# Rotary swap by ScalarE copies instead of a TensorE product, and a new placement of the buffers in SBUF

## The chip, the cores and the metric

The kernel runs on one core of a Trainium2 chip. The metric is the device time of one execution in microseconds (us). An execution works on both input sequences, through both layers of the encoder.

## What is computed

The reference is an encoder of two layers on two sequences of 256 tokens, with 1024 features. Each layer has one input projection; its columns feed a windowed attention with rotary positions and a two-sided state-space mixer (SSD). An output projection, a layer norm, a gated MLP and a second layer norm follow. All data is float32. The part that the change touches is the rotation:

```python
def rope(x):                      # x (B,S,H,64), for 8 query heads and 2 key heads
    ang = arange(s)[:, None] * inv_freq[None, :]
    cos, sin = cos(ang), sin(ang)
    x1, x2 = x[..., :32], x[..., 32:]
    return concatenate([x1 * cos - x2 * sin, x2 * cos + x1 * sin], -1)

def hybrid_layer(h, ...):
    proj = h @ w_in
    q, k, v, z, xbc, dt_raw = split(proj)
    attn_out = window_attention(rope(q), rope(k), v, sink)
    ...                           # conv, SiLU, SSD, gate, RMS norm
    h = layer_norm(ALPHA * h + concat(attn_out, ssd_out) @ w_out)
    gate, val = split(h @ w_up)
    return layer_norm(ALPHA * h + (silu(conv(gate)) * val) @ w_down)
```

## The kernel before, in words

**Units.** The weights of a layer are cut into 105 units of 128x1024: unit 0 is the time step (dt), 1 the keys, 2 the values, 3 to 6 the queries (two heads each), 7 to 18 the columns that go through the convolution, 19 to 26 the gate z, 27 to 38 the output projection, 39 to 82 the MLP's first product, 83 to 104 its second. SyncE loads them into a ring of five (`raw`). ScalarE rounds each to float32r (`whi`, L554), VectorE takes the rest (`wlo`, L1113), which overwrites `raw`. Each float32 product is three float32r matmuls: high by high, high by low, low by high. The activations are kept in the same two parts (`hhi`/`hlo`, `ahi`/`alo`, `uhi`/`ulo`).

**Two forms of the big product.** `by_columns` (L778 to L780) has 128 columns of `whi` or `wlo` as the stationary operand and 512 tokens of `hhi` or `hlo` as the moving one: 24 matmuls a unit, all into one PSUM bank. `by_rows` (L821 to L823; output projection and the MLP's second product) has 128 tokens of `ahi`, `alo`, `uhi` or `ulo` as the stationary operand and 512 columns of `whi` or `wlo` as the moving one. `first_units` runs the first two units after a layer norm with 256 tokens at a time.

**Order.** `mixer_schedule` writes one list of steps, which every engine walks and from which it takes its own: G (a unit on TensorE), E (ScalarE empties that unit's bank), S (split of the unit four ahead), ROT (rotation), DTT and SP (softplus of dt), AA, AO and SM (the decay sums, their matmuls and their split), VT (transposes of the values), AS, AM, AX, AD, AN, AP, AV (attention, from step 8 on), F, F2 and SILU (convolution taps and SiLU). The engines run apart and meet at semaphores. G(i) waits until unit i-2 has been emptied. VT takes the PSUM bank of AA, so it waits until VectorE has written `own_z` from it (L1289).

**Rotation before.** For each of five tiles of 128 rows (two heads), ScalarE copies the bank to `qk` (L651). TensorE multiplies `qk` by the 128x128 matrix `rot` (L975; a plain float32 matmul, which the profile counts as two), which puts minus the upper 32 rows of each head where the lower are, and the lower where the upper are. VectorE multiplies that product by the sines into `ropet` (L1328), `qk` by the cosines (L1329), and adds (L1331). `rope_done` counts finished tiles. ROT stands one step behind its unit.

**Buffers.** They are allocated one after another. Without an alignment asked for, each starts at the next multiple of 32 bytes. In the program before, in bytes per partition: `cn` (constants) at 16512, `avg` at 21792, `raw`/`wlo` at 23488, `whi` at 43968, `hhi` at 64448, `hlo` at 80832, `big_i` at 100096, the two arenas at 101632 and 118016. The other tiles (`ahi`, `alo`, `uhi`, `ulo`, `own_w`, `heads`, `qk`, ...) lie at whole multiples of 1024 bytes in an arena. All slots and slices of the big operands step by multiples of 512 bytes. So `whi`, `wlo`, `hhi`, `hlo` start 960 bytes past a multiple of 2048, the tiles at even KB of the arenas 1280 past one, and `avg` 32 past a multiple of 64.

Of the kernel before, what the change touches and what calls it, by code (L numbers as in the profile page):

```python
# [61 lines left out]
def _columns(table, widths):  # L62
    at = 0
    for name, w in widths:
# [11 lines left out]
                     ("before", P), ("rot", P), ("cos", SEQ), ("sin", SEQ),  # L76
# [28 lines left out]
def mixer_schedule():  # L105
    steps = []
    for n in range(U_OUT):
        i = n - A0
        steps += [("G", n), ("E", n)]
        if 0 <= i < 8:  # L110
            steps += [("AS", i), ("AM", i)]
        if 0 <= i - 2 < 8:
            steps += [("AV", i - 2)]
        if n == 1:
            steps += [("DTT", 0), ("SP", 0)]
        if n == 3:
            steps += [("AA", 0), ("AO", 0), ("SM", 0)]
        if n - 1 == U_V:
            steps += [("VT", 0)]
        if n - 1 == U_K:  # L120
            steps += [("ROT", 4)]
        if U_Q <= n - 1 < U_Q + 4:
            steps += [("ROT", n - 1 - U_Q)]
        steps += [("S", n + AHEAD)]
        if 0 <= i < 8:
            steps += [("AX", i)]
        steps += [("F", n)]
        if 0 <= i < 8:
            steps += [("AD", i), ("AN", i)]
        if n == 15:  # L130
            steps += [("MV", 0), ("MV", 1)]
        if n == 16:
            steps += [("MV", 2), ("MV", 3)]
        if U_CONV <= n < U_Z:
            steps += [("F2", n)]
        if 0 <= i - 1 < 8:
            steps += [("AP", i - 1)]
        j = n - 1 - U_CONV
        if 4 <= j < N_CONV:
            steps += [("T", j)]  # L140
        if 12 <= n < 16:
            steps += [("CB", n - 12)]
        if U_CONV <= n < U_Z:
            steps += [("SILU", n - U_CONV)]
            if n - U_CONV >= 4:
                steps += [("XS", n - U_CONV)]
        for k in PROD_SLOTS.get(n, []):
            steps += prod_steps(k)
        if n == 23:
            steps += [("SG", i) for i in range(3)]  # L150
        if n == 24:
            steps += [("SG", 3)]
        if n == 26:
            steps += [("SG", i) for i in range(4, 7)] + [("SQ", c) for c in range(4)]
# [27 lines left out]
def trunk(nc, x_in, units, pm_d, pf_d, cn_d, gb_d, h_d, y_d):  # L182
    ctx = ExitStack()
    with ctx:
# [7 lines left out]
        cn = sb("cn", [P, CN_W])  # L192
        avg = sb("avg", [P, P])

        st = sb("st", [P, NBLK, 4])
        pm = sb("pm", [P, PM_W])
        pf = sb("pf", [P, PF_W])
# [5 lines left out]
        dt = sb("dt", [P, NBLK, 32])  # L203
        cum_a = sb("cum_a", [P, TOK])
        neg_a = sb("neg_a", [P, 32])
        ast = sb("ast", [P, 2, 6, QPK])

        big_i = sb("big_i", [P, P], F32R)
        cut = sb("cut", [P, 2, P], F32R)
# [6 lines left out]
        base = nc.sbuf_base - ARENA_KB * KB  # L216

# [79 lines left out]
        proj_copied, rope_sin, rope_done = sem("proj_copied"), sem("rope_sin"), sem("rope_done")  # L297
# [33 lines left out]
        for what, i in SCHED:  # L331
# [15 lines left out]
            elif what == "ROT":  # L347
                aux(("ROT", i), [(rope_sin, 5, (i + 1) % 5 + 1)])
            elif what == "AP":
                yy(("AP", i, 0), [(pt_done, 8, i + 1)])  # L350
                yy(("AP", i, 1), [(pt_done, 8, i + 1)])
            elif what == "AV":
                aux(("AV", i), [(al_done, 8, i + 1)])
            elif what == "RS" and i == 0:
                aux(("RS", 0), [(rms_std, 1, 1)], False)
            elif what == "SD":
                aux(("SD", i), [(y_sum, 8, i + 1)])
# [189 lines left out]
        def _(act):  # L547
# [81 lines left out]
            for L in range(DEPTH):  # L629
                act.wait_ge(pm_loaded, L * 16 + 16)  # L630
                for what, i in SCHED:
# [15 lines left out]
                    elif what == "E" and i < U_Z:  # L647
                        m = i - U_K
                        act.wait_ge(unit_used, L * UNITS + i + 1)
                        dst = zt[:] if i == U_V else qk[:, 4 if i == U_K else i - U_Q, :]  # L650
# [122 lines left out]
        def _(pe):  # L773
# [94 lines left out]
            for L in range(DEPTH):  # L868
                for what, i in SCHED:
# [102 lines left out]
                    elif what == "ROT":  # L972
                        pe.wait_ge(proj_copied, L * 6 + (1 if i == 4 else 3 + i))
                        wait_aux_free(pe, L, (what, i))
                        mm(ps[:, aux_bank((what, i)), :], cst("rot"), qk[:, i, :], start=True,  # L975
                           stop=True).then_inc(aux_full, 1)
# [129 lines left out]
        def _(dve):  # L1106
# [103 lines left out]
            for L in range(DEPTH):  # L1210
                dve.wait_ge(pm_loaded, L * 16 + 16)
                for what, i in SCHED:
# [107 lines left out]
                    elif what == "ROT":  # L1320
                        wait_aux_full(dve, L, (what, i))
# [3 lines left out]
                        r = ps[:, aux_bank((what, i)), :].rearrange("p (b s) -> p b s", b=NSEQ)  # L1325
                        if n:
                            dve.wait_ge(rope_done, L * 5 + n)
                        V.tensor_tensor(tt, r, cst("sin").unsqueeze(1).broadcast_to((P, NSEQ, SEQ)), ALU.mult).then_inc(rope_sin, 1)  # L1328
                        chain(V.tensor_tensor(x, x, cst("cos").unsqueeze(1).broadcast_to((P, NSEQ, SEQ)), ALU.mult))  # L1329
                        dve.wait_ge(rope_sin, L * 5 + n + 1)  # L1330
# [131 lines left out]
def constants():  # L1462
# [3 lines left out]
    rot = np.zeros((P, P), np.float32)  # L1466
    for m in range(P):
        if m % HEAD < HEAD // 2:
            rot[m + HEAD // 2, m] = -1.0
        else:  # L1470
            rot[m - HEAD // 2, m] = 1.0
    freq = np.float32(10000.0) ** (-np.arange(0, HEAD, 2, dtype=np.float32) / np.float32(HEAD))
    ang = np.arange(SEQ, dtype=np.float32)[None, :] * freq[np.arange(P) % (HEAD // 2)][:, None]
    row = np.arange(P)
    is_a = (row // 16) % 2 == 1
# [5 lines left out]
        "after": k > q, "before": k < q, "rot": rot, "cos": np.cos(ang), "sin": np.sin(ang),  # L1481
# [77 lines left out]
```

## Time and profile before

| | us |
|---|---|
| median of three runs | 1392.52 (1392.41 to 1395.36) |
| the profiled execution | 1392.02 |
| its span, first to last instruction | 1390.2 |
| busy in the span: PE (matmul) | 1355.3 (97%) |
| PEld (weight load) | 1102.4 |
| VectorE (DVE) | 754.6 |
| ScalarE (ACT) | 559.6 |
| GpSimd (POOL) | 202.4 |

A matmul's record reaches from its start to the end of its way through the array, and the next one starts before it ends. So the busy time of PE says that it is rarely idle, not how fast it goes. How fast is read from the distance between starts, or from the count of matmuls in a window in which PE doesn't wait.

### The profile page before, as it was taken

How to read it: one execution, taken by the hardware profiler on the slowest of the kernel's cores; microseconds unless marked ns; L12 is line 12 of the kernel's file. 1: busy time of each engine (PE TensorE's matmuls, PEld its weight loads, DVE VectorE, ACT ScalarE, POOL GpSimd, SP SyncE). 2: the span in 40 equal slices, each digit the busy share in tenths (PEclk: the TensorE clock that was granted, in tenths of full speed). 3: DMA queues.
4: the chain of work that ended last, by engine and by line, in shares of the span. 5: the costliest groups of instructions: out<-in, count | busy, mean ns of one | idle time of the engine just before them, and what ended most of it. 6: DMA issues, size and time to landing. Idle time of an engine off the chain costs nothing.

```text
span 1390.2 us, 16378 instructions
## 1 busy us (share of the span) xinstructions
PE 1355.3 (97%) x6740; PEld 1102.4 (79%) x6740; DVE 754.6 (54%) x1006; ACT 559.6 (40%) x851; POOL 202.4 (15%) x119
## 2 busy tenths in 40 slices
PE   7999999999999999999999999999999999999997
PEld 6777778788888888888777777877788888888886
DVE  5777776655544444332266877667464444443225
ACT  5355544425433333311253655444263333333112
POOL 3013400162000000060020224002520000002300
PEclk9999999999999999999999999999999999999999
DMA  4421111251333333333224221124233333333332
GB/s 160 152 76 60 48 60 46 63 193 48 117 95 93 105 91 98 114 106 91 76 95 137 61 62 61 46 61 161 67 95 103 91 103 95 93 104 121 91 94 103
DMA packets 33786, 129.95 MB, mean 93 GB/s; under 512 B 3792, under 2 KB 3952, under 8 KB 32560
## 3 DMA queue, kind: packets, MB, share of 16 engines
q1 hardware_dynamic: 33552, 128.61, 29.4%
q8 instruction: 54, 0.88, 0.3%
q0 software_dynamic: 160, 0.29, 0.1%
q14 instruction: 20, 0.16, 0.0%
HBM read 122.60 MB, written 6.29 MB: 93 GB/s over the span
## 4 chain that ended last, share of the span: by engine, by line
PE 86%; DVE 6%; ACT 4%; issue 2%; DMA 1%; POOL 1%; DVEq 0%; SPq 0%; ACTq 0%; POOLq 0%
PE ps L778 17%; PE ps L780 17%; PE ps L779 17%; PE ps L821 8%; PE ps L823 8%; PE ps L822 8%; PE ps L1015 2%; DVE cv L1226 1%; PE ps L995 1%; ACT junk L559 1%; PE ps L1046 1%; PE ps L1056 1%; DVE hb L1128 1%; DVE wlo L1113 1%; PE ps L1036 1%
## 5 line engine op out<-in xcount | busy, mean ns | idle before, releaser
L778 PE MATMUL ps<-hhi,whi 128*128 128x512 f32 (+1 forms) x1200 | 464.9, 387 | 11.4 <-DVE hlo L1161 10.5
L779 PE MATMUL ps<-hlo,whi 128*128 128x512 f32 (+1 forms) x1200 | 455.8, 380 | 0.0
L780 PE MATMUL ps<-hhi,wlo 128*128 128x512 f32 (+1 forms) x1200 | 455.7, 380 | 0.0
L1113 DVE TENSOR_TENSOR wlo<-raw,whi 128x1024 fp32r<-128x1024 f32 x210 | 272.8, 1300 | 272.0 <-ACT whi L554 271.8
L554 ACT ACTIVATE whi<-raw 128x1024 fp32r<-128x1024 f32 x210 | 221.2, 1054 | 237.2 <-DMA raw<-in_units 237.2
L778 PEld LDWEIGHTS ps<-hhi,whi 128*128 128x128 f32 x1200 | 228.0, 190 | 58.4 <-DVE hlo L1161 7.6
L779 PEld LDWEIGHTS ps<-hlo,whi 128*128 128x128 f32 x1200 | 228.3, 190 | 43.5 <-issue 2.4
L780 PEld LDWEIGHTS ps<-hhi,wlo 128*128 128x128 f32 x1200 | 228.1, 190 | 42.6
L821 PE MATMUL ps<-whi,uhi 128*128 128x512 f32 x352 | 139.4, 396 | 0.0
L822 PE MATMUL ps<-whi,ulo 128*128 128x512 f32 x352 | 139.2, 395 | 0.0
L823 PE MATMUL ps<-wlo,uhi 128*128 128x512 f32 x352 | 139.2, 395 | 0.0
L1411 DVE SCALAR_TENSOR_TENSOR gcv<-ps,pf,gcv 128x510 f32<-128x510 f32 x44 | 33.0, 749 | 160.7 <-ACT gcv L749 160.5
L749 ACT ACTIVATE gcv<-ps,pf 128x512 f32<-128x512 f32 x44 | 34.2, 777 | 175.0 <-PE ps L780 175.0
L480 POOL TENSOR_TENSOR hb<-hb,gb 128x1024 f32<-128x1024 f32 x8 | 20.9, 2642 | 500.2 <-DMA gb<-in_gb 500.2
L821 PE MATMUL ps<-whi,ahi 128*128 128x512 f32 x192 | 77.6, 404 | 2.1 <-DVE wlo L1113 1.9
L821 PEld LDWEIGHTS ps<-whi,uhi 128*128 128x128 f32 x352 | 66.2, 188 | 15.9
L823 PEld LDWEIGHTS ps<-wlo,uhi 128*128 128x128 f32 x352 | 66.2, 188 | 15.9
L822 PEld LDWEIGHTS ps<-whi,ulo 128*128 128x128 f32 x352 | 66.2, 188 | 15.9
L822 PE MATMUL ps<-whi,alo 128*128 128x512 f32 x192 | 75.9, 395 | 0.0
L823 PE MATMUL ps<-wlo,ahi 128*128 128x512 f32 x192 | 75.9, 395 | 0.0
L1421 DVE TENSOR_TENSOR guf<-gsg,ps 128x512 f32<-128x512 f32 x44 | 30.2, 687 | 83.1 <-PE ps L780 82.5
L1226 DVE SCALAR_TENSOR_TENSOR cv<-ps,pm,cv 128x508 f32<-128x508 f32 (+1 forms) x96 | 71.4, 743 | 2.5
(170 smaller groups left out, 1413.0 us busy)
## 6 DMA issues: line engine op xcount, KB each, us to landing
raw<-in_units SPq DMA_DIRECT2D x210, 512.0 KB, 3.6
gb<-in_gb SPq DMA_DIRECT2D x5, 1024.0 KB, 5.6
h_kept<-hb SPq DMA_DIRECT2D x2, 2048.0 KB, 9.3
ha<-h_kept SPq DMA_DIRECT2D x2, 2048.0 KB, 10.0
hb<-in_x SPq DMA_DIRECT2D x4, 512.0 KB, 6.3
out_y<-hb SPq DMA_DIRECT2D x8, 256.0 KB, 2.0
cn<-in_cn SPq DMA_DIRECT2D x1, 585.5 KB, 9.6
pm<-in_pm POOLq DMA_DIRECT2D x2, 80.0 KB, 3.5
```

The lines of the kernel that those rows point to most:

```text
L554: A(whi[:, m % RING, :], raw[:, m % RING, :], ACT.Copy).then_inc(unit_hi, 1)
L749: A(gcv[:], ps[:, bank, :], ACT.Identity, scale=pf[:, k * 3 + w0 + 1:k * 3 + w0 + 2], bias=pf[:, k + v0:k + v0 + 1]).then_inc(glu_center, 1)
L778: mm(out, whi[:, slot, cols], xhi, start=start, stop=False)
L779: mm(out, whi[:, slot, cols], xlo, start=False, stop=False)
L780: return mm(out, wlo[:, slot, cols], xhi, start=False, stop=stop)
L821: mm(ps[:, bank, :], xhi[:, rows], whi[:, slot, cols], start=start, stop=False)
L822: mm(ps[:, bank, :], xlo[:, rows], whi[:, slot, cols], start=False, stop=False)
L823: return mm(ps[:, bank, :], xhi[:, rows], wlo[:, slot, cols], start=False, stop=stop)
L1113: V.tensor_tensor(wlo[:, m % RING, :], raw[:, m % RING, :], f(whi[:, m % RING, :]), ALU.subtract).then_inc(unit_split, 1)
L1226: V.scalar_tensor_tensor(out=dst[:, :, lo:hi], in0=src[:, :, lo + s:hi + s], scalar=pmc("conv_w", 5 * j + tap, 5 * j + tap + 1), in1=dst[: ...
L1411: V.scalar_tensor_tensor(out=dst[:, :, 1:SEQ], in0=src[:, :, 0:SEQ - 1], scalar=pf[:, k * 3 + w0:k * 3 + w0 + 1], in1=dst[:, :, 1:SEQ], op ...
L1421: V.tensor_tensor(guf[:], gsg[:], ps[:, bank + 1, :], ALU.mult).then_inc(glu_done, 1)
```

## The change

- The `rot` matrix and its products are gone. ScalarE writes the rotated partner itself: four copies of 32 rows each from the unit's PSUM bank to `ropet`, row group q from row group q^1, and then the copy to `qk`. The sign is put into the table of sines. VectorE multiplies `ropet` by the sines in place.
- ScalarE waits for `rope_done` of the tile before, since all tiles share `ropet`.
- ROT stands at its own unit's step instead of one step behind.
- The rotation takes no bank of PSUM any more.
- A padding tensor `to_step` is placed ahead of `raw`, and the small tensors are allocated behind the arenas.

In the built program after the change `to_step` stands at 16512 and `raw`/`wlo` at 18464, `whi` at 38944, `hhi` at 59424, `hlo` at 75808, the arenas at 92192 and 108576, `cn` at 217120, `big_i` at 226464. The big operands and the even KB of the arenas all start 32 bytes past a multiple of 2048.

```diff
-                     ("before", P), ("rot", P), ("cos", SEQ), ("sin", SEQ),
+                     ("before", P), ("cos", SEQ), ("sin", SEQ),
...
-        if n - 1 == U_K:
+        if n == U_K:
             steps += [("ROT", 4)]
-        if U_Q <= n - 1 < U_Q + 4:
-            steps += [("ROT", n - 1 - U_Q)]
+        if U_Q <= n < U_Q + 4:
+            steps += [("ROT", n - U_Q)]
...
-        cn = sb("cn", [P, CN_W])
-        avg = sb("avg", [P, P])
-
-        st = sb("st", [P, NBLK, 4])
-        pm = sb("pm", [P, PM_W])
-        pf = sb("pf", [P, PF_W])
+        STEP = 2048
+        sb("to_step", [P, -(-nc.sbuf_base // STEP) * STEP - nc.sbuf_base], mybir.dt.uint8)
         raw = sb("raw", [P, RING, 1024])
...
         arena = sb("arena", [P, ARENA_KB * KB // 4])
         base_h = nc.sbuf_base - ARENA_KB * KB - CT * TOK * 4
         base = nc.sbuf_base - ARENA_KB * KB
+
+        cn = sb("cn", [P, CN_W])
+        avg = sb("avg", [P, P])
+        st = sb("st", [P, NBLK, 4])
...
-            elif what == "ROT":
-                aux(("ROT", i), [(rope_sin, 5, (i + 1) % 5 + 1)])
...
                         act.wait_ge(unit_used, L * UNITS + i + 1)
+                        if i != U_V:
+
+                            if i != U_K:
+                                act.wait_ge(rope_done, L * 5 + i - U_Q + 1)
+                            for q in range(4):
+                                A(ropet[32 * q:32 * q + 32, :], ps[32 * (q ^ 1):32 * (q ^ 1) + 32, unit_bank(i), :],
+                                  ACT.Copy).then_inc(rope_swapped, 1)
                         dst = zt[:] if i == U_V else qk[:, 4 if i == U_K else i - U_Q, :]
                         A(dst, ps[:, unit_bank(i), :], ACT.Copy).then_inc(proj_copied, 1)
...
-                    elif what == "ROT":
-                        pe.wait_ge(proj_copied, L * 6 + (1 if i == 4 else 3 + i))
-                        wait_aux_free(pe, L, (what, i))
-                        mm(ps[:, aux_bank((what, i)), :], cst("rot"), qk[:, i, :], start=True,
-                           stop=True).then_inc(aux_full, 1)
...
                     elif what == "ROT":
-                        wait_aux_full(dve, L, (what, i))
                         n = (i + 1) % 5
...
-                        if n:
-                            dve.wait_ge(rope_done, L * 5 + n)
-                        V.tensor_tensor(tt, r, cst("sin").unsqueeze(1).broadcast_to((P, NSEQ, SEQ)), ALU.mult).then_inc(rope_sin, 1)
+                        dve.wait_ge(rope_swapped, L * 20 + 4 * n + 4)
+                        chain(V.tensor_tensor(tt, tt, cst("sin").unsqueeze(1).broadcast_to((P, NSEQ, SEQ)), ALU.mult))
+                        dve.wait_ge(proj_copied, L * 6 + (1 if i == 4 else 3 + i))
                         chain(V.tensor_tensor(x, x, cst("cos").unsqueeze(1).broadcast_to((P, NSEQ, SEQ)), ALU.mult))
-                        dve.wait_ge(rope_sin, L * 5 + n + 1)
                         V.tensor_tensor(qk[:, i, :], qk[:, i, :], ropet[:], ALU.add).then_inc(rope_done, 1)
...
-        "after": k > q, "before": k < q, "rot": rot, "cos": np.cos(ang), "sin": np.sin(ang),
+        "after": k > q, "before": k < q, "cos": np.cos(ang), "sin": sign * np.sin(ang),
```

Two engines change their order. On ScalarE, from the keys (unit 1) to the decay sums' copy `own_hi`, stood before:

```order
L651 ACTIVATE qk<-ps 128x512 [waits unit_used]
L672 ACT_TABLE_LOAD
L672 ACTIVATE sp<-sp 128x128 [waits dt_abs]
L673 ACTIVATE neg_a<-pm 128x32
L675 ACT_TABLE_LOAD
L675 ACTIVATE sp<-sp 128x128 [waits dt_floor]
L554 ACTIVATE whi<-raw 128x1024 [waits raw_loaded0]
L651 ACTIVATE zt<-ps 128x512 [waits unit_used]
L554 ACTIVATE whi<-raw 128x1024 [waits raw_loaded1]
L651 ACTIVATE qk<-ps 128x512 [waits unit_used]
L678 ACTIVATE own_hi<-ps 128x512 [waits aux_full]
```

The same stretch of ScalarE after the change, where `sp` is softplus's scratch and `zt` the values:

```order
L654 ACTIVATE ropet<-ps 32x512 [waits unit_used]
L654 ACTIVATE ropet<-ps 32x512 x3
L657 ACTIVATE qk<-ps 128x512
L678 ACT_TABLE_LOAD
L678 ACTIVATE sp<-sp 128x128 [waits dt_abs]
...
L657 ACTIVATE zt<-ps 128x512 [waits unit_used]
L553 ACTIVATE whi<-raw 128x1024 [waits raw_loaded1]
L654 ACTIVATE ropet<-ps 32x512 [waits rope_done,unit_used]
L654 ACTIVATE ropet<-ps 32x512 x3
L657 ACTIVATE qk<-ps 128x512
L684 ACTIVATE own_hi<-ps 128x512 [waits aux_full]
```

Four copies now stand ahead of softplus's exponential, and four more, with a wait for `rope_done`, ahead of `own_hi`. On VectorE, from the end of softplus to the decay sums, stood before:

```order
L1282 TENSOR_TENSOR ln_dt<-sp 128x16x16 [waits dt_log]
L1113 TENSOR_TENSOR wlo<-raw,whi 128x1024 [waits unit_hi]
L1328 TENSOR_TENSOR ropet<-ps,cn 128x512 [waits aux_full]
L1329 TENSOR_TENSOR qk<-qk,cn 128x512
L1331 TENSOR_TENSOR qk<-qk,ropet 128x512 [waits rope_sin,dve_link]
L1113 TENSOR_TENSOR wlo<-raw,whi 128x1024 [waits unit_hi]
L1289 SCALAR_TENSOR_TENSOR own_z<-own_hi,cn,ps 128x512 [waits own_high]
```

And VectorE there after the change:

```order
L1283 TENSOR_TENSOR ln_dt<-sp 128x16x16 [waits dt_log]
L1326 TENSOR_TENSOR ropet<-ropet,cn 128x512 [waits rope_swapped]
L1328 TENSOR_TENSOR qk<-qk,cn 128x512 [waits proj_copied,dve_link]
L1329 TENSOR_TENSOR qk<-qk,ropet 128x512 [waits dve_link]
L1114 TENSOR_TENSOR wlo<-raw,whi 128x1024 [waits unit_hi] x2
L1290 SCALAR_TENSOR_TENSOR own_z<-own_hi,cn,ps 128x512 [waits own_high]
```

The rotation of the keys has moved ahead of a split and reads ScalarE's copies, not TensorE's product.

## Rows read from the trace of the kernel before

**Rows 1.** The page, busy time: engine, us, share of the span, instructions.
```profile
PE 1355.3 (97%) x6740; PEld 1102.4 (79%) x6740; DVE 754.6 (54%) x1006; ACT 559.6 (40%) x851; POOL 202.4 (15%) x119
```

**Rows 2.** Waits of PE in the whole span: total us, times, longest.
```profile
PE ps L969 <- DVE own_z L1289: 1.4, 2, 0.7
PE ps L1046 <- POOL sc L503: 1.2, 2, 0.6
```

**Rows 3.** Windows: length, busy us (count) of PE, PEld, DVE, ACT, POOL; clock, DMA.
```profile
360.00:560.00 200.00, 200.00 (x884) 165.60 (x883) 91.37 (x109) 73.71 (x92) 0.00 (x0) 1.00 0.33 97
580.00:690.00 110.00, 110.00 (x473) 88.63 (x472) 28.35 (x23) 21.03 (x21) 21.86 (x8) 1.00 0.32 101
1366.00:1381.00 15.00, 15.00 (x66) 12.10 (x65) 10.82 (x18) 4.21 (x8) 0.00 (x0) 1.00 0.19 71
```

**Rows 4.** Groups of instructions by shape: count, busy us, mean ns, idle before.
```profile
L780 PE MATMUL ps<-hhi,wlo 128*128 128x512 f32 x1072 | 417.4, 389 | 0.0
...
L821 PE MATMUL ps<-whi,uhi 128*128 128x512 f32 x352 | 139.4, 396 | 0.0
...
L821 PE MATMUL ps<-whi,ahi 128*128 128x512 f32 x192 | 77.6, 404 | 2.1 <-DVE wlo L1113 1.9
```

**Rows 5.** Timeline of PE around two rotation products: start, duration, instruction.
```profile
63.63 1.02 PE L975 MATMUL ps<-qk,cn 128*128 128x512 f32 x2
64.09 0.80 PE L778 MATMUL ps<-hhi,whi 128*128 128x512 f32 x1
...
69.96 1.02 PE L975 MATMUL ps<-qk,cn 128*128 128x512 f32 x2
```

**Rows 6.** Timeline of ACT, units 0 and 1.
```profile
34.15 0.59 ACT L636 ACTIVATE zt<-ps 32x512 f32<-32x512 f32 x1 [3.07 <-PE ps L780]
34.64 1.04 ACT L554 ACTIVATE whi<-raw 128x1024 fp32r<-128x1024 f32 x1
35.59 0.57 ACT L651 ACTIVATE qk<-ps 128x512 f32<-128x512 f32 x1
...
37.57 0.31 ACT L672 ACTIVATE sp<-sp 128x128 f32<-128x128 f32 x1
```

**Rows 7.** Timeline of DVE, end of softplus to the decay sums.
```profile
43.94 0.42 DVE L1282 TENSOR_TENSOR ln_dt<-sp 128x256 f32<-128x256 f32 x1
...
45.76 0.68 DVE L1328 TENSOR_TENSOR ropet<-ps,cn 128x512 f32<-128x512 f32 x1
...
47.08 0.69 DVE L1331 TENSOR_TENSOR qk<-qk,ropet 128x512 f32<-128x512 f32 x1
...
50.47 0.75 DVE L1289 SCALAR_TENSOR_TENSOR own_z<-own_hi,cn,ps 128x512 fp32r<-128x512 f32 x1 [1.56 <-ACT own_hi L678]
```

**Rows 8.** Timeline of ACT, unit 3 and the decay sums.
```profile
47.89 0.60 ACT L651 ACTIVATE qk<-ps 128x512 f32<-128x512 f32 x1 [1.88 <-PE ps L780]
49.84 0.60 ACT L678 ACTIVATE own_hi<-ps 128x512 fp32r<-128x512 f32 x1 [1.35 <-PE ps L933]
```

**Rows 9.** Timeline of PE, transposes of the values and start of unit 4.
```profile
51.36 0.63 PE L969 MATMUL ps<-cn,zt 128*128 128x128 f32 x4 [0.69 <-DVE own_z L1289]
51.74 0.48 PE L778 MATMUL ps<-hhi,whi 128*128 128x512 f32 x1
```

**Rows 10.** Timeline of PE, matmuls of 256 tokens: first sequence, then second.
```profile
336.07 0.28 PE L778 MATMUL ps<-hhi,whi 128*128 128x256 f32 x1
336.19 0.28 PE L779 MATMUL ps<-hlo,whi 128*128 128x256 f32 x1
...
340.56 0.28 PE L780 MATMUL ps<-hhi,wlo 128*128 128x256 f32 x1
340.68 0.28 PE L778 MATMUL ps<-hhi,whi 128*128 128x256 f32 x1
```

**Rows 11.** Timeline of PE, plain float32 matmuls, each window's rows merged.
```profile
6.65 1.73 PE L861 MATMUL ps<-avg 128*128 128x128 f32 x14
...
24.33 1.04 PE L813 MATMUL ps<-cn,hb 128*128 128x128 f32 x8
...
264.95 1.88 PE L1070 MATMUL ps<-sqr,avg 128*128 128x512 f32 x4
```

More of the change, by code:

```diff
@@ L189, in sem @@
             return ctx.enter_context(nc.semaphore(name))
+        STEP = 2048
+        sb("to_step", [P, -(-nc.sbuf_base // STEP) * STEP - nc.sbuf_base], mybir.dt.uint8)
+        raw = sb("raw", [P, RING, 1024])
+        wlo = nc.alloc_sbuf_tensor_at("wlo", [P, RING, 1024], F32R, offset=nc.sbuf_base - RING * 4096)
+        whi = sb("whi", [P, RING, 1024], F32R)
+        hhi = sb("hhi", [P, CT, TOK], F32R)
+        hlo = sb("hlo", [P, CT, TOK], F32R)
+        KB = 1024
+        ARENA_KB = 106
+        arena_h = sb("arena_h", [P, CT * TOK])
+        arena = sb("arena", [P, ARENA_KB * KB // 4])
+        base_h = nc.sbuf_base - ARENA_KB * KB - CT * TOK * 4
+        base = nc.sbuf_base - ARENA_KB * KB
         cn = sb("cn", [P, CN_W])
@@ L197, in trunk @@
         pf = sb("pf", [P, PF_W])
-        raw = sb("raw", [P, RING, 1024])
-        wlo = nc.alloc_sbuf_tensor_at("wlo", [P, RING, 1024], F32R, offset=nc.sbuf_base - RING * 4096)
-        whi = sb("whi", [P, RING, 1024], F32R)
-        hhi = sb("hhi", [P, CT, TOK], F32R)
-        hlo = sb("hlo", [P, CT, TOK], F32R)
         dt = sb("dt", [P, NBLK, 32])
@@ L209, in trunk @@
         cut = sb("cut", [P, 2, P], F32R)
-        KB = 1024
-        ARENA_KB = 106
-        arena_h = sb("arena_h", [P, CT * TOK])
-        arena = sb("arena", [P, ARENA_KB * KB // 4])
-        base_h = nc.sbuf_base - ARENA_KB * KB - CT * TOK * 4
-        base = nc.sbuf_base - ARENA_KB * KB
         def at(name, kb, shape, dtype=F32, start=None):
@@ L296, in trunk @@
         aux_full, t_evac, cb_done = sem("aux_full"), sem("t_evac"), sem("cb_done")
-        proj_copied, rope_sin, rope_done = sem("proj_copied"), sem("rope_sin"), sem("rope_done")
+        proj_copied, rope_swapped, rope_done = sem("proj_copied"), sem("rope_swapped"), sem("rope_done")
         v_done, tanh_done, zs_done = sem("v_done"), sem("tanh_done"), sem("zs_done")
@@ L1324, in _ @@
                         x = qk[:, i, :].rearrange("p (b s) -> p b s", b=NSEQ)
-                        r = ps[:, aux_bank((what, i)), :].rearrange("p (b s) -> p b s", b=NSEQ)
-                        if n:
-                            dve.wait_ge(rope_done, L * 5 + n)
-                        V.tensor_tensor(tt, r, cst("sin").unsqueeze(1).broadcast_to((P, NSEQ, SEQ)), ALU.mult).then_inc(rope_sin, 1)
+                        dve.wait_ge(rope_swapped, L * 20 + 4 * n + 4)
+                        chain(V.tensor_tensor(tt, tt, cst("sin").unsqueeze(1).broadcast_to((P, NSEQ, SEQ)), ALU.mult))
+                        dve.wait_ge(proj_copied, L * 6 + (1 if i == 4 else 3 + i))
                         chain(V.tensor_tensor(x, x, cst("cos").unsqueeze(1).broadcast_to((P, NSEQ, SEQ)), ALU.mult))
-                        dve.wait_ge(rope_sin, L * 5 + n + 1)
                         V.tensor_tensor(qk[:, i, :], qk[:, i, :], ropet[:], ALU.add).then_inc(rope_done, 1)
@@ L1465, in constants @@
     q = np.arange(P)[None, :]
[L1466 to L1471, printed above, removed]
     freq = np.float32(10000.0) ** (-np.arange(0, HEAD, 2, dtype=np.float32) / np.float32(HEAD))
@@ L1474, in constants @@
     row = np.arange(P)
+    sign = np.where(row % HEAD < HEAD // 2, np.float32(-1), np.float32(1))[:, None]
     is_a = (row // 16) % 2 == 1
```

## The prediction

> **What bounds the kernel now.** I read the busy times first: PE is busy 97% of the span, the next engine 54% [rows 1]. Then the list of PE's waits: most of them are at the layer norms, which the change doesn't touch, and those near it are 1.4 us for `own_z` and 1.2 us for GpSimd's `sc` [rows 2]. So time is won only where TensorE has fewer or faster instructions, or where one of these waits goes; it is lost where PE gets a new wait.
>
> PE's speed is then read from windows in which it never waits. In 360 to 560 us (all `by_columns`) 884 matmuls are counted; a window also counts the record that reaches in from the left, so the distance of starts is (200 + 0.39) / 884 = 226.7 ns. In 580 to 690 us (all `by_rows`) it is (110 + 0.39) / 473 = 233.4 ns [rows 3, 4]. Both move 512 columns at a granted clock of 1.00, that is 2.4 GHz, where 512 columns take 213.3 ns. So each matmul carries 13.3 ns on top in one form and 20.0 in the other. That is worth attention, since there are 3 x 1072 = 3216 of the first and 3 x (352 + 192) = 1632 of the second [rows 4].
>
> **The change part by part: the product leaves PE.** From one rotation product to the next, with one unit between, PE needs 69.96 - 63.63 = 6.33 us [rows 5]. 24 matmuls at 226.7 ns are 5.44. A rotation product costs 0.89 us of PE, with nothing beside it. Ten of them are 8.9 us.
>
> For the keys' product this doesn't count directly, because PE waits a little later anyway, for `own_z`. I follow that chain in absolute times, in layer 1.
>
> **The four copies.** The trace has no copy from one row group to another. The nearest row is the 32x512 copy from PSUM at 0.59 us, as long as the 128x512 one at 0.57 to 0.60 [rows 6, 8]: fewer rows make it no shorter. Copies with no wait between them overlap: the one that starts at 34.64 takes 1.04 and the next starts at 35.59, 0.09 early [rows 6]. I take 0.50 us a copy; the bounds are 0.40 (a deeper overlap) and 1.18 (a copy across row groups at twice the price).
>
> - Unit 1: softplus's exponential starts at 37.57 [rows 6] and now at 39.57, behind 4 x 0.50. Softplus on VectorE ends at 44.36 [rows 7], now at 46.36.
> - The keys' rotation follows at once instead of after a split. It took 45.76 to 47.77 [rows 7]; with a link after the first multiplication I take 2.1 us, so `rope_done` comes at 48.5.
> - Unit 3 ends on PE 0.89 earlier than the 47.89 at which its copy starts [rows 8], at 47.0, but ScalarE now waits for `rope_done` until 48.5. Four copies and the one to `qk` end at about 51.0, and `own_hi` starts there instead of at 49.84. AA is done on PE by 49.0 and doesn't bind.
> - `own_z` starts 1.16 us later than 50.47 [rows 7], at 51.63. The transposes and unit 4 follow: unit 4 starts at 52.9, not 51.74 [rows 9].
>
> From there PE runs on. Unit 6 needs unit 4's bank: unit 4's copies wait for the first query rotation, which stands behind the decay sums on VectorE and is done near 59.3, so the bank is free near 61.9; unit 6 starts at 63.8. The slack is 1.9 us, and it grows by a unit's remainder each time (5.44 us of PE against some 5.1 us of copies and rotation in sequence). The splits on both engines are queued behind the waiting copies, but they are for units four ahead. So each layer gains 4 x 0.89 - 1.16 = 2.4 us, both 4.8. Bounds: 8.9 if the copies delay nothing; with copies of 0.59 it is 3.2; at 1.18 the wait before unit 4 grows to 6.4 us and units 6 and 7 wait too, and a layer loses some 5 us, both 10.
>
> **A wait that goes.** VectorE did the convolution of unit 7 behind the last rotation, and attention's first block with it; GpSimd's `sc` came 0.6 us late for PE once a layer. VectorE is now about 3 us ahead there. I take the whole 1.2 us [rows 2]; bounds 0 and 1.2. PE's waits at the norms stay.
>
> **The placement.** What distinguishes 226.7 from 233.4? Not the PSUM bank: `by_rows` changes it after three matmuls, but in the last three units nine in a row go to one bank, and there 66 matmuls in 15.39 us are 233.2 ns apart as well [rows 3]. The moving operand starts 960 past a multiple of 2048 in both forms. Only the stationary one differs: 960 past in `by_columns`, 1280 in `by_rows`. So the pace hangs on the stationary operand's place, alone or against the moving one's. After the change both operands of both forms start 32 past. Against each other they then lie as in `by_columns` today (a multiple of 512 apart). If that is what counts, `by_rows` falls to 226.7: 1632 x 6.7 ns = 10.9 us less. I take that. Bounds are what rows allow: every matmul at `by_rows`'s pace costs 3216 x 6.7 = 21.5 us; at the best pace in the trace (below) 62.5 us are won.
>
> The sum is 1392.0 - 4.8 - 1.2 - 10.9 = 1375.1 us, against the profiled execution's 1392.02 (span 1390.2 and 1.8 around it), which is 0.5 below the median of the runs. I say 1375.
>
> **Rivals.**
>
> *Placement does nothing.* The matmuls of 256 tokens speak for it: they start 120 ns apart in both sequences [rows 10], although the first reads within a 2048-byte block and the second across its edge, so crossing an edge costs nothing and the two forms may differ for a reason I don't see. All starts are multiples of 32 bytes before and after. Then 1392.0 - 6.0 = 1386.0. The Trainium skill speaks for this rival: its page "SBUF — State Buffer" (section on Door 1, the DMA port swizzle) has lines of 16 bytes as the unit in which access is fast or slow, and both layouts start on one. It leaves the two paces unexplained.
>
> *Slower: every read starts inside a 64-byte block.* The placement misses a multiple of 2048 by 32. Before, all big operands started on a multiple of 64; after, none does. In the trace one matmul has both operands there, the one on `avg`: 14 records in 1.73 us with 0.28 for the last are 111.5 ns apart, while those on `hb` are 1.04 - 0.28 over 7, 109 ns [rows 11]. If that 2.5 ns came with each big product, it would cost 12 us; if it brings all to `by_rows`'s pace, 21.5. Time 1398 to 1407, I take 1402. It ends slower than before as soon as it costs more than 6.0 / 4848 = 1.2 ns a matmul. Against it: with only the stationary operand on `avg`, four float32 matmuls are (1.88 - 0.59) / 3 = 430 ns apart, close to the 426.7 that 1024 cycles take [rows 11].
>
> *Everything falls to the floor.* Those 430 ns show a matmul with only some 3 ns on top. If the 13 and 20 ns are all due to placement, the 4848 matmuls come to 216 ns: 3216 x 10.7 + 1632 x 17.4 = 62.8 us less, 1323. Rows 10 speak against it: the 256-token matmuls carry the same 13.3 ns (120 - 106.7), so it is a cost per matmul. The Trainium skill has this floor too: "TensorE: Matmul & The Clock Gate" (section "Wait — 56ns, not 53.3ns?") gives N/2.4 GHz plus about 2.5 ns, 215.7 ns for 512 columns. The trace's float32r matmuls don't agree, at 226.7 and 233.4.
>
> *The copies stall PE.* At 1.18 us a copy the rotation loses 10 us instead of winning 4.8; with the by-rows gain the time is 1390, without it 1401. The two rows of 0.59 speak against it. Its chance is in the range, not a case of its own.
>
> **How the numbers follow.** Forecast (by_rows at the other form's pace, 1375) 0.42; placement does nothing (1386) 0.25; slower by the 64-byte start (1402) 0.20; to the floor, or a good part of the way (1323 to 1365) 0.13. The range 1366 to 1399 holds the first two with their bounds for the rotation (1 to 3 us each way), and the mild end of the third. What is left out is most of the fourth and the heavy half of the third. This kernel's measurement tells 0.2%, 2.8 us, from no change. Faster holds the first, most of the second, which would need 3.2 us more to fail, and the fourth: 0.75. Same takes 0.07, slower 0.18.
>
> **What would show it.** Right: in the windows of the MLP's second product the distance of starts is 226.7 ns, and unchanged in the first product; unit 4 of layer 1 starts near 52.9 and PE's wait for `own_z` has grown from 0.7 to about 2.7 us a layer; units 4 to 7 follow at 5.44 us; the wait for `sc` is gone; a swapped copy is 0.59 long. Wrong: a distance in `by_columns` other than 226.7, in either direction, which takes the placement term with it; a wait of PE for ScalarE's `qk` before unit 6; the copies longer than 0.6 us.

## The result and the profile after

The changed kernel takes 1384.34 us (median of 4 runs, 1384.17 to 1386.27) against 1392.84 us (median of 4, 1392.41 to 1395.36) for the kernel before on the same chip: ratio 0.9938, 95% interval 0.9921 to 0.9956. It is faster by 8.5 us, half of the 17 I forecast. 1384.3 lies inside the range, but the sum behind 1375 is wrong by 9 us.

The profiled execution took 1386.27 us, its span 1384.4. The page's busy line, in the columns of [rows 1]:

```profile
PE 1341.7 (97%) x6720; PEld 1102.4 (80%) x6720; DVE 765.0 (55%) x1006; ACT 583.4 (42%) x891; POOL 202.1 (15%) x119
```

Twenty matmul records fewer (ten products, two each) and forty ScalarE copies more. PE is busy for 13.6 us less, but the span fell by 5.8: it waits more. The list of PE's waits, against [rows 2]:

```profile
PE ps L784 <- DVE hlo L1162: 10.3, 5, 3.7
PE ps L975 <- DVE own_z L1290: 7.3, 2, 3.6
PE ps L1016 <- DVE e_off L1343: 4.7, 2, 2.4
...
PE ps L827 <- ACT std L741: 1.7, 2, 0.9
...
PE ps L1047 <- POOL sc L502: 1.1, 2, 0.5
```

The wait for `own_z` grew from 0.7 to 3.65 us a layer (forecast 2.7), and the wait for `sc`, which I had gone, is still 0.5 of its 0.6. The wait of `by_rows` (L827) for `std`, the root that ScalarE computes for the RMS norm at the output projection, is new: the list of the kernel before has none. Windows, in the columns of [rows 3]:

```profile
360.00:560.00 200.00, 200.00 (x884) 165.58 (x884) 92.55 (x110) 73.45 (x91) 0.00 (x0) 1.00 0.31 98
580.00:690.00 110.00, 110.00 (x487) 91.10 (x486) 29.85 (x25) 22.76 (x23) 21.83 (x8) 1.00 0.32 101
...
54.00:62.00 8.00, 6.20 (x18) 5.09 (x19) 6.90 (x15) 3.05 (x6) 0.00 (x0) 0.57 0.40 171
733.00:741.00 8.00, 6.27 (x18) 5.10 (x19) 6.97 (x15) 2.98 (x6) 0.00 (x0) 0.57 0.45 188
```

The first row is `by_columns` with the same 884 matmuls: 226.7 ns, unchanged. The second is `by_rows`: 487 for 473, (110 + 0.39) / 487 = 226.7 ns, down from 233.4. The last two are news: just behind the wait for `own_z` the granted clock is 0.57 in both layers, that is, mostly 1.2 GHz and not 2.4. ScalarE's timeline from the keys to the decay sums (start, duration, instruction, idle before), against [rows 6, 8]:

```profile
38.02 2.44 ACT L654 ACTIVATE ropet<-ps 32x512 f32<-32x512 f32 x4
40.49 0.60 ACT L657 ACTIVATE qk<-ps 128x512 f32<-128x512 f32 x1
41.10 1.28 ACT L678 ACT_TABLE_LOAD   x1
42.40 0.31 ACT L678 ACTIVATE sp<-sp 128x128 f32<-128x128 f32 x1
...
51.33 2.43 ACT L654 ACTIVATE ropet<-ps 32x512 f32<-32x512 f32 x4 [0.49 <-DVE qk L1329]
53.78 0.60 ACT L657 ACTIVATE qk<-ps 128x512 f32<-128x512 f32 x1
54.28 0.59 ACT L684 ACTIVATE own_hi<-ps 128x512 fp32r<-128x512 f32 x1
```

Four swapped copies take 2.44 us, 0.61 each: they don't overlap at all, while `own_hi` starts 0.50 behind a `qk` copy of 0.60. (That they are short of rows isn't the reason: the 32-row copy to `zt`, which keeps its rows, starts at 36.47 and lasts 0.59, and the next instruction starts at 36.96.) The Trainium skill's page "ScalarE: Activation LUTs" (section "What ACT_TABLE_LOAD costs") lets instructions back to back overlap by about 93 ns; the 0.10 of the last two rows agrees, the four copies do not. VectorE and PE next, against [rows 7, 9]:

```profile
49.10 0.68 DVE L1326 TENSOR_TENSOR ropet<-ropet,cn 128x512 f32<-128x512 f32 x1
...
54.90 0.75 DVE L1290 SCALAR_TENSOR_TENSOR own_z<-own_hi,cn,ps 128x512 fp32r<-128x512 f32 x1 [1.40 <-ACT own_hi L684]
```

```profile
55.80 1.09 PE L975 MATMUL ps<-cn,zt 128*128 128x128 f32 x4 [3.65 <-DVE own_z L1290]
56.54 0.78 PE L784 MATMUL ps<-hhi,whi 128*128 128x512 f32 x1
57.11 0.63 PE L785 MATMUL ps<-hlo,whi 128*128 128x512 f32 x1
57.54 0.63 PE L786 MATMUL ps<-hhi,wlo 128*128 128x512 f32 x1
```

Behind the wait the matmuls of unit 4 start 430 ns apart, close to the 426.7 of 512 columns at 1.2 GHz. The clock is recorded as halved from 54.7 to 61.5 us, and from 733.9 to 740.8 in layer 2.

**Where the time went.** Starts of units in both profiled executions, in us, split the difference:

| stretch | before | after | difference |
|---|---|---|---|
| start to unit 2, layer 1 | 35.8 | 38.1 | +2.3 |
| unit 2 to 9, layer 1 (the rotation) | 48.2 | 49.5 | +1.25 |
| unit 9 to unit 2 of layer 2 | 634.9 | 629.5 | -5.4 |
| unit 2 to 9, layer 2 | 48.2 | 49.6 | +1.4 |
| unit 9 to the end | 623.1 | 617.8 | -5.3 |

The sum is -5.8, the difference of the spans. The +2.3 is a second stretch of 1.2 GHz in the start-up (27.4 to 34.2 us); this execution was the slowest of the four by about that much, so it isn't charged to the change. The rotation, forecast to win, costs 2.6.

The two long stretches hold all 1632 `by_rows` matmuls, and their -10.7 looks like the placement's term. It is a sum of four things, though. The parts with `by_rows` matmuls are 9.7 us shorter. In both layers PE meets the new wait, 0.87 us each, 1.7 together:

```profile
270.06 1.02 PE L1071 MATMUL ps<-rms_sum,avg 128*128 128x512 f32 x2
271.95 0.47 PE L827 MATMUL ps<-whi,ahi 128*128 128x512 f32 x1 [0.87 <-ACT std L741]
```

The end, behind the last `by_rows` matmul, is 0.4 longer. And the execution before had 1.2 GHz for 3.4 us at 341 and at 1024 us, each time 1.5 us more for the same matmuls, while this one had it at neither: -3.0.

The new wait comes from banks. Small products take PSUM banks 6 and 7 in turn. Without the five rotation products a layer the sum for the RMS norm is the 33rd to take one and not the 38th, so by the kernel's code it lies in bank 6, before in bank 7. `by_rows` goes through bank 6 first and may not write it until ScalarE has read the sum into `std`. Before, three matmuls into bank 6 ran meanwhile. Every trace without rotation products has this wait of 0.87 (the changed kernel and experiments 2 to 7), and none with them. Another order of the banks wasn't tried.

In layer 1 the +1.25 is made up so. Measured from the start of unit 2, `own_z` starts 16.8 us later for 14.7 before: +2.1. The transposes and unit 4 then run at 1.2 GHz: 0.74 us from the transposes' start to unit 4's for 0.38 [rows 9], and unit 4 lasts 7.88 us; with full clock it lasts 5.57 (experiments below). That is +2.7, and in layer 2, where unit 4 lasts 8.02, +2.8. The products that left give back 3.5.

### The profile page after: what moved, and what is told of

The parts are those of the page before. It is cut to its first block, busy times and chain, and to the rows that moved or that the text cites. A ratio compares the mean times of both kernels' runs of the same rounds, so it can differ in the third digit from the quotient of the medians.

```text
span 1384.4 us, 16368 instructions
## 1 busy us (share of the span) xinstructions
PE 1341.7 (97%) x6720; PEld 1102.4 (80%) x6720; DVE 765.0 (55%) x1006; ACT 583.4 (42%) x891; POOL 202.1 (15%) x119
## 4 chain that ended last, share of the span: by engine, by line
PE 83%; DVE 7%; ACT 5%; issue 2%; DMA 1%; POOL 1%; DVEq 0%; SPq 0%; ACTq 0%; POOLq 0%
PE ps L784 17%; PE ps L786 17%; PE ps L785 17%; PE ps L827 8%; PE ps L828 8%; PE ps L829 8%; PE ps L1016 2%; DVE cv L1227 1%; PE ps L996 1%; ACT junk L558 1%; PE ps L1047 1%; ACT whi L553 1%; PE ps L1057 1%; DVE hb L1129 1%; DVE wlo L1114 1%
## 5 line engine op out<-in xcount | busy, mean ns | idle before, releaser
L1114 DVE TENSOR_TENSOR wlo<-raw,whi 128x1024 fp32r<-128x1024 f32 x210 | 281.8, 1343 | 260.9 <-ACT whi L553 260.7
L827 PE MATMUL ps<-whi,uhi 128*128 128x512 f32 x352 | 137.1, 390 | 0.0
L827 PE MATMUL ps<-whi,ahi 128*128 128x512 f32 x192 | 75.7, 394 | 3.7 <-DVE wlo L1114 2.0
L827 PEld LDWEIGHTS ps<-whi,uhi 128*128 128x128 f32 x352 | 66.1, 188 | 13.8
```

The lines of the kernel that those rows point to most:

```text
L827: mm(ps[:, bank, :], xhi[:, rows], whi[:, slot, cols], start=start, stop=False)
L1114: V.tensor_tensor(wlo[:, m % RING, :], raw[:, m % RING, :], f(whi[:, m % RING, :]), ALU.subtract).then_inc(unit_split, 1)
```

## The experiments

Ratios are to the kernel before on the same chip, with their 95% interval.

**1 and 2. The two halves apart.** First the placement alone, with the rotation still a product:

```diff
-        cn = sb("cn", [P, CN_W])          # ... and the other small tensors
+        sb("to_step", [P, -(-nc.sbuf_base // STEP) * STEP - nc.sbuf_base], mybir.dt.uint8)
         raw = sb("raw", [P, RING, 1024])
...
         base = nc.sbuf_base - ARENA_KB * KB
+        cn = sb("cn", [P, CN_W])          # ... and the others, here
```

> The kernel before with the new placement alone: raw, whi, hhi, hlo and both arenas start 32 bytes past a multiple of 2048, the small tensors behind them, the rotation still a TensorE product. Theory (the pace of the big matmuls hangs on where the stationary operand lies against the moving one): by_rows starts 226.7 ns apart instead of 233.3, by_columns 226.7 as before, so 1632 x 6.7 ns = 10.9 us less, 1381.9 us, and no fall of the clock near unit 4. Rival (the pace changed by something that the rotation brought): by_rows stays at 233.3 and the time near 1392.8.

Measured: 1382.62 us (1380.16 to 1383.88), ratio 0.9919 (0.9903 to 0.9934), 10.4 us less. The window of the MLP's second product:

```profile
580.00:680.00 100.00, 100.00 (x443) 82.81 (x442) 26.42 (x19) 20.15 (x19) 21.81 (x8) 1.00 0.34 106
```

(100 + 0.39) / 443 = 226.6 ns. The wait for `own_z` is 0.7 as before. Then the rotation alone, at the addresses of the kernel before (a dummy of 512 bytes stands in for the table that left):

> The changed kernel with every big buffer at its old address (a dummy tensor of 512 bytes fills the place of rot). Theory (ScalarE's copies in front of the decay sums cost more than the product saves): per layer +2.5 us between units 2 and 4, +2.5 us of half clock behind PE's wait of 3.65 us, -3.55 us over units 4 to 7, in all +1.4 a layer, so 1392.8 + 2.8 = 1395.6 us. Rival (the rotation wins and the placement won only a few us): below 1390. Second rival (my forecast's sum): 1388.0 without the half clock.

Measured: 1393.33 us (1390.08 to 1397.74), ratio 0.9998 (0.9985 to 1.0011). Again 233.4 ns, a wait of 3.6 us for `own_z`, and 1.2 GHz from 53.2 to 60.0 and 739.2 to 746.1. I had expected 2.8 us more than before; measured are 0.3, inside the interval. So the whole gain is the placement's, and the rotation, ten products lighter, wins nothing.

**3 and 5. Is it the clock?** If the half clock is the answer to PE's wait, products that fill the wait must restore it, though they do nothing useful. `FILL` products of `avg` by itself stand ahead of the transposes:

```diff
+                        for _ in range(FILL):
+                            mm(ps[:, 4, 0:P], avg[:], avg[:], start=True, stop=True)
```

FILL = 32:

> The changed kernel with 32 matmuls of avg by avg (128 columns, plain float32, near 0.11 us each, 3.6 us) into an unused PSUM bank in front of the transposes of the values, where PE waits 3.65 us a layer. They compute nothing that is used. Theory (PE's standing still lets the clock fall to 1.2 GHz behind it): no fall near units 4 and 5, period of unit 4 down from 7.9 to 5.5 us, 4.9 us less than the changed kernel, 1379.4 us. Rival (the clock falls for another reason, or the filler delays the transposes): 1384.3 or more.

Measured: 1389.78 us (1388.25 to 1390.7), ratio 0.997 (0.9959 to 0.9981). I had made the filler twice too long, since each product counts as two matmuls:

```profile
51.01 7.41 PE L974 MATMUL ps<-avg 128*128 128x128 f32 x64
```

It covers 7.4 us where 3.7 were idle, and the transposes start 3.5 us later than in the changed kernel, measured from unit 2. But unit 4 now takes 5.57 us, not 7.88, at a clock of 1.00. FILL = 16:

> As e3_filled_wait with 16 filler products instead of 32. In e3 each plain float32 product was two matmuls of 0.11 us, so 32 of them took 7.4 us and outlasted the wait of 3.65 us; 16 take 3.7. They compute nothing that is used. Theory (PE's standing still for 3.65 us makes the clock fall behind it): unit 4's period is 5.57 us as in e3, unit 2 to unit 4 stays near 18.5 us, and the time is near 1379.5 us, 4.9 below the changed kernel's 1384.3. Rival (the clock's two falls cost less than their periods show, since falls elsewhere take their place): 1382 to 1384.

Measured: 1380.88 us (1379.06 to 1383.24), ratio 0.9915 (0.9901 to 0.9929). The window behind the wait, against 0.57 above, and the filler:

```profile
54.00:62.00 8.00, 8.00 (x42) 6.79 (x42) 7.80 (x16) 2.40 (x5) 0.00 (x0) 1.00 0.30 124
```

```profile
51.03 3.84 PE L974 MATMUL ps<-avg 128*128 128x128 f32 x32
...
54.76 0.63 PE L978 MATMUL ps<-cn,zt 128*128 128x128 f32 x4
```

Unit 4 lasts 5.55 us. Useless work on an idle engine made the kernel about 3.5 us faster (3.2 by the ratios); the half clock after the wait is shown to be its price. On the spot the filler wins 5.5 us over both layers. The total is less, as the recorded rival had it: in this execution the clock is at 1.2 GHz from 185.1 to 188.5 and from 864.3 to 867.7, where the changed kernel's was whole, and that costs 1.6 us each time.

**4. The copies out of the way.** The four copies become ScalarE's part of the step ROT, behind `qk`'s copy and from it:

```diff
-                            for q in range(4):
-                                A(ropet[32 * q:32 * q + 32, :], ps[32 * (q ^ 1):32 * (q ^ 1) + 32, unit_bank(i), :],
-                                  ACT.Copy).then_inc(rope_swapped, 1)
...
+                    elif what == "ROT":
...
+                        for q in range(4):
+                            A(ropet[32 * q:32 * q + 32, :], qk[32 * (q ^ 1):32 * (q ^ 1) + 32, i, :],
+                              ACT.Copy).then_inc(rope_swapped, 1)
```

> The changed kernel with ScalarE's swapped copies as a step of their own at ROT's place in the list: behind softplus for the keys and behind the decay sums for the first queries; they read qk in SBUF instead of the PSUM bank. Theory (the cost was that the copies stood in front of softplus's exponential and of own_hi): PE's wait for own_z is back at 0.7 to 0.9 us, the clock doesn't fall there, and all ten products' 0.89 us are won: 1392.8 - 10.9 - 8.5 = 1373.4 us. Rival (the copies cost ScalarE too much wherever they stand, and later units wait for their banks): PE waits for ScalarE at units 4 to 7, 1380 or more.

Measured: 1378.09 us (1376.28 to 1379.78), ratio 0.9885 (0.9867 to 0.9904). PE's wait and the first matmul behind it, with the clock whole in the window:

```profile
51.90 0.63 PE L976 MATMUL ps<-cn,zt 128*128 128x128 f32 x4 [1.73 <-DVE own_z L1291]
52.28 0.47 PE L785 MATMUL ps<-hhi,whi 128*128 128x512 f32 x1
```

```profile
54.00:62.00 8.00, 8.00 (x37) 6.62 (x36) 6.30 (x12) 6.57 (x10) 0.00 (x0) 1.00 0.41 148
```

That is 4.7 us more than expected. The wait went to 1.73 and not to 0.7 to 0.9, which is some 2 us over both layers. A wait of 1.73 us did not cost the clock; the one of 3.65 did. Read from SBUF a copy takes 0.65 (2.60 for four), yet from the start of unit 2 to that of unit 8 it is 38.0 us for 42.6. The rest of the miss stands elsewhere. The wait for `std` is there as in the changed kernel, 1.7 us, and at the end of the wait for `e_off` (2.4 us) the clock now halves for 3.4 us in both layers, as it did in the placement-only run at 862 us, and unit 19 takes 14.5 us instead of 13.0.

**6. Still further behind.** Keys' rotation at step 3, each query's one step later:

```diff
-        if n == U_K:
+        if n == 3:
             steps += [("ROT", 4)]
-        if U_Q <= n < U_Q + 4:
-            steps += [("ROT", n - U_Q)]
+        if U_Q <= n - 1 < U_Q + 4:
+            steps += [("ROT", n - 1 - U_Q)]
```

> As e4_copies_behind, with every rotation one step later and the keys' rotation at step 3, behind the decay sums and the transposes of the values, so that nothing of the rotation stands ahead of own_hi on either engine. Theory (what was left of the cost in e4 was the keys' copies ahead of the split and own_hi, 1.7 us of wait a layer instead of 0.7): wait for own_z 0.7 us, unit 2 to unit 4 is 15.5 us instead of 16.1, 1.2 us less than e4, near 1377 us. Rival (the tight chain of ropet over ScalarE and VectorE now reaches attention, which waits for rope_done): PE waits at step 8, 1378 or more.

Measured: 1384.3 us (1382.84 to 1387.82), ratio 0.994 (0.9923 to 0.9957), 7 us above what I expected. The waits of PE name the new one:

```profile
PE ps L785 <- DVE cv L1228: 5.5, 2, 2.8
...
PE ps L976 <- DVE own_z L1291: 1.4, 2, 0.7
```

`own_z` is as early as in the kernel before, but the last query's rotation now stands ahead of the first convolution taps on VectorE:

```profile
76.51 0.69 DVE L1327 TENSOR_TENSOR ropet<-ropet,cn 128x512 f32<-128x512 f32 x1 [2.35 <-ACT ropet L675]
...
79.82 3.17 DVE L1228 SCALAR_TENSOR_TENSOR cv<-ps,pm,cv 128x508 f32<-128x508 f32 x4
```

All five tiles share `ropet`, so copies and arithmetic alternate, some 4.8 us a tile. Delayed by a step, the chain holds up the taps of unit 7, and TensorE may not start unit 9 until they have emptied its bank. Moving work off one wait made another of 2.8, again with a stretch of 1.2 GHz behind it (82.0 to 88.8 us).

**7. One split out of the way.** In experiment 4 VectorE runs two splits, 2.35 us, just ahead of `own_z`. The one of unit 6 goes behind the first query's rotation:

```diff
-        steps += [("S", n + AHEAD)]
+        if n == 3:
+            steps += [("S", 2 + AHEAD)]
+        if n != 2:
+            steps += [("S", n + AHEAD)]
```

> The version with the copies behind ROT's place (1378.1 us, wait for own_z 1.7 us a layer), with the split of unit 6 moved from unit 2's step to unit 3's, behind the first rotation. There VectorE ran two splits, 2.35 us, until 51.09 between the keys' rotation and own_z, while own_hi was done at 50.13. If the order on VectorE is what holds the transposes of the values: own_z starts at 50.1 to 50.2 and not at 51.0, the wait falls from 1.7 to about 0.85 us a layer, unit 4 starts 0.9 earlier, time 1378.1 - 1.8 = 1376.3. If ScalarE's copies hold it (own_hi later by as much), the wait stays at 1.7 and the time at 1378. If the split is then late for unit 6, a wait before unit 6 or 7 shows and the time is above 1378.

Measured: 1376.73 us (1374.77 to 1377.61), ratio 0.9879 (0.9857 to 0.99). The time is 0.4 from the 1376.3 expected here; the ratios of this run and experiment 4 overlap. The mechanism is in the trace:

```profile
PE ps L979 <- DVE own_z L1294: 1.4, 2, 0.7
```

The wait is 0.7 us a layer as before the change, and from unit 2 to unit 8 it is 36.9 us for 38.0. This is the fastest version run: 16 us below the kernel before.

**8 to 12. What is it about the placement?** These have the rotation as a product. By how many bytes the stationary operand starts past the moving one, mod 512, is what the theory goes by. Their diffs are paddings. Run 8 is the kernel before with 320 bytes ahead of `raw` and 1728 ahead of the arenas, which puts everything 1280 past a multiple of 2048. The others start from experiment 1: run 9 has 320 bytes ahead of the arenas, and runs 10 and 11 have

```diff
+        sb("gap0", [P, 320], mybir.dt.uint8)   # ahead of hhi; 256 in run 11
         hhi = sb("hhi", [P, CT, TOK], F32R)
...
+        sb("gap", [P, 256], mybir.dt.uint8)    # ahead of arena_h; 384 in run 11
         arena_h = sb("arena_h", [P, CT * TOK])
```

Run 12 has `to_step` of 1920 bytes, which puts all on a true multiple of 2048.

> The kernel before (rotation on TensorE) with raw, whi, hhi, hlo and the arenas all 1280 bytes past a multiple of 2048, by two gaps. Theory (what counts is the distance of stationary and moving operand modulo 512): it is 0 in both forms, both forms start 226.7 ns apart. Rival (the stationary operand's own place counts): it is 1280 in both, as in by_rows before, so both forms run at 233.3, 1392.8 + 21 = 1414 us.

> e1_place_only with the arenas moved by 320 bytes: raw, whi, hhi, hlo 32 past a multiple of 2048, the arenas 352. Theory (distance): in by_rows the stationary operand lies 320 past the moving one modulo 512, as in the kernel before, so by_rows starts 233.3 ns apart, by_columns 226.7. Rival (the stationary operand's own place): 352 is neither 960, 32 nor 1280, so 233.3 would be chance; 226.7 in by_rows speaks against the distance.

> The kernel before with the new placement, but the activations hhi/hlo another 320 bytes on and the arenas 576 bytes on from whi/wlo. Stationary minus moving start, mod 512: 192 in the first product's form (by_columns), 64 in by_rows; no distance so far was among these (only 0 and 320 were). If any distance other than 0 costs the same: by_columns 233.3 ns and by_rows 233.3, time 1382.6 + 3216 x 6.6 ns + 1632 x 6.6 = 1414.7. If the cost grows with the distance to the nearest multiple of 512 (320 has 192): by_columns as at 320, 233.3, by_rows between 226.7 and 233. If only 320 is bad: both 226.7 and 1382.6. If the stationary operand's own place counts and not the distance: by_columns unchanged at 226.7.

> The same with two more distances mod 512: 256 in by_columns, 128 in by_rows. Any distance other than 0 the same: both 233.3, 1414.7. Cost by distance to the nearest multiple of 512: by_columns (256) at least 233.3, by_rows (128) below that. Only 320 bad: both 226.7, 1382.6.

> The kernel before with the new placement, but all big operands at a true multiple of 2048 bytes, where the change stops 32 bytes past one. If a start in the middle of a 64-byte block costs nothing, as the 226.7 ns of both forms suggest, this is the run of placement alone again: both forms 226.7 ns, 1382.6 (ratio 0.992). If the 32 bytes do cost something, the distances fall below 226.7; at 1 ns a product that is 4.8 us, 1377.8 (ratio 0.989).

The windows of `by_columns` and `by_rows` in run 10, and of `by_rows` in runs 9 and 11:

```profile
360.00:560.00 200.00, 200.00 (x876) 164.09 (x874) 91.94 (x110) 72.95 (x90) 0.00 (x0) 1.00 0.33 97
580.00:690.00 110.00, 110.00 (x473) 88.18 (x472) 25.95 (x22) 22.32 (x22) 21.80 (x8) 1.00 0.33 104
```

```profile
580.00:690.00 110.00, 110.00 (x473) 88.62 (x472) 27.87 (x22) 21.22 (x20) 21.87 (x8) 1.00 0.32 101
```

```profile
580.00:690.00 110.00, 110.00 (x475) 89.20 (x474) 29.15 (x23) 21.45 (x21) 21.88 (x8) 1.00 0.32 101
```

| run | time, us | `by_columns`: distance, ns | `by_rows`: distance, ns |
|---|---|---|---|
| before | 1392.8 | 0, 226.7 | 320, 233.4 |
| 1, placement alone | 1382.6 | 0, 226.7 | 0, 226.6 |
| 8, all 1280 past 2048 | 1381.8 (one run) | 0, 226.7 | 0, 226.6 |
| 9, arenas +320 | 1395.8 (one run) | 0, 226.7 | 320, 233.4 |
| 10 | 1399.3 (one run) | 192, 228.8 | 64, 233.4 |
| 11 | 1395.2 (one run) | 256, 226.7 | 128, 232.4 |
| 12, true 2048 | 1382.2 | 0, 226.7 | 0, 227.1 |

(The `by_rows` values of runs 1, 8 and 12 are from the window 580 to 680 us, where one matmul more or less in the count is 0.5 ns.) Run 12's ratio is 0.9913 (0.9894 to 0.9933). Run 8 puts the operands where `by_rows` was slow, and both are fast: not the own place. Run 9 brings the slow pace back by moving one operand. Run 12 shows that the 32 bytes past a multiple cost nothing. The distance decides, but not by either rule that I had written down for runs 10 and 11: 256 is as good as 0, 192 costs 2.1 ns, 64, 128 and 320 cost 5.7 to 6.7. The rows fit a period of 256 bytes just as well as one of 512 (320 is 64 past 256, and both give 233.4); no run tells the two apart. Since the two forms were never run at the same distance but 0, the form may have a part in it.

## Why the prediction was wrong

- **Placement, -10.9: right.** The pace fell from 233.4 to 226.7 ns, the time by 10.4 us with the placement alone; in the changed kernel's execution the parts with these matmuls are 9.7 us shorter. The reading of [rows 3], that the distance between the operands sets the forms apart, held: at distance 0 both run at 226.7. Both rivals about the placement's effect (nothing, or a cost from the start in a 64-byte block) are out, as is the fall to the floor. (The bound that the prediction gives once as 62.5 and once as 62.8 us is 62.8.)
- **"I take 0.50 us a copy": mis-sized.** They took 0.61. I carried an overlap over from copies that keep their rows [rows 6]. The 0.59 that I also worked through was the better value. Two batches of four stand ahead of `own_z`: 8 x 0.11 = 0.9, and `own_z` came 2.1 us later, not 1.16. Over both layers this is 1.9 us. (Softplus's exponential starts 4.29 us after unit 2 and not 1.78: 2.5 for the 2.0 taken.)
- **"The transposes and unit 4 follow ... From there PE runs on": the failed step.** I let PE's wait cost its own length. Behind it the transposes and unit 4 ran at 1.2 GHz: 2.7 us in layer 1 and 2.8 in layer 2, 5.5 us, which no term held. Experiments 3 and 5 show it by restoring the clock, experiment 4 by shortening the wait.
- **"PE's waits at the norms stay": a second step that failed.** The new wait for `std` costs 0.87 us a layer, 1.7 in all. That the rotation takes no bank of PSUM any more was on the list of changes, and the prediction put it at nothing.
- **"I take the whole 1.2 us": wrong.** Only 0.1 went. VectorE's taps of unit 7 wait behind a split that stands ahead of them in its order, that split waits for ScalarE's, and ScalarE's stands behind the copy from unit 7's bank. First ScalarE, then VectorE:

```profile
80.94 0.78 ACT L644 ACTIVATE cv<-ps,pm 128x512 f32<-128x512 f32 x1 [1.44 <-PE ps L786]
```

```profile
80.02 1.22 DVE L1114 TENSOR_TENSOR wlo<-raw,whi 128x1024 fp32r<-128x1024 f32 x1
82.69 1.23 DVE L1114 TENSOR_TENSOR wlo<-raw,whi 128x1024 fp32r<-128x1024 f32 x1 [1.46 <-ACT whi L553]
83.95 3.17 DVE L1227 SCALAR_TENSOR_TENSOR cv<-ps,pm,cv 128x508 f32<-128x508 f32 x4
```

  So the taps start 3.0 us behind the end of unit 7 on TensorE, for 3.9 before. But TensorE has no rotation product behind unit 7 any more and is 0.9 earlier too, so the wait hardly changes. This is read from the traces and wasn't tried.
- **The products, 0.89 each: right** for the three in between, as units 5 to 7 each take 5.44 us for 6.33 [rows 5]. No wait for `qk` before unit 6 appeared.

The sum with what the two profiled executions show: 1375.1 + 1.9 (copies) + 5.5 (clock behind the wait) + 1.7 (`std`) + 1.2 (`sc`) + 1.2 (`by_rows`, 9.7 for 10.9) + 0.4 (the end) = 1387.0. The start-up with its second stretch of 1.2 GHz adds 2.3, and the stretches missing at 341 and 1024 us take off 3.0: 1386.3, against 1386.27. The other three executions of the changed kernel took 2 us less; they weren't traced. So by this estimate the failed steps alone would have brought the time to 1387, and that the median came out near 1384 is in part the clock's doing, which the forecast didn't hold.

## What to carry to other kernels

A wait on TensorE is priced by its length and by the clock behind it; here 3.65 us of waiting cost 2.7 more, and 1.73 cost nothing. Work taken from the bound engine and given to one that feeds it has to be placed by what is queued behind it there: the same five rotations a layer were worth nothing as first placed, and 4.5 and 5.9 us against the placement alone in experiments 4 and 7, by their place in ScalarE's and VectorE's order. Where products take two banks in turn, removing an odd number of them gives every later one the other bank: ask who waits for which. And operand addresses are worth a look when two forms of the same matmul differ in pace.

## What the hardware showed that I had not expected

- The pace of 512-column float32r matmuls depends on the distance mod 512 between the starts of the two operands: 226.7 ns at 0 and 256, 228.8 at 192, 232.4 to 233.4 at 64, 128 and 320. A multiple of 2048 itself, 32 past it and 1280 past it are alike. A period of 256 fits these numbers too. The Trainium skill's page "SBUF — State Buffer" (section "Operand start alignment") asks only for element alignment and says of its runs that they timed nothing; on speed these windows decide.
- ScalarE copies of 32 rows from PSUM to other rows cost 0.61 us each back to back, more than 128 rows in their own place at 0.50.
- Where the clock falls varies: the traced execution of the kernel before had 1.2 GHz for 3.4 us at 341 and 1024, the changed one at neither, the placement-only one at 862. Each such stretch moves 1 to 1.6 us, so two versions that differ elsewhere can differ by that. In the traces of the five kernels whose `by_rows` runs at 232 to 233 ns, 9 of these 10 places have such a stretch; in the nine at 227 ns, 2 of 18. So the pace may have a part in it; how isn't shown. Executions of one kernel differ as well: 20 of the kernel before took 1390.8 to 1397.1 us, with mean granted clocks of 0.995 in the fastest and 0.990 in the slowest.
